# Rotary halves on VectorE, norm factors behind the products, and the second block's two attentions in one pipeline of heads

## The reference, cut to what matters

```python
def rmsnorm(x, g):
    y = xf * lax.rsqrt(jnp.mean(xf * xf, axis=-1, keepdims=True) + EPS)
    return (y * g.astype(F32)).astype(x.dtype)

def rope(x, pos):                     # x1, x2: the two halves of a head's features
    return jnp.concatenate([x1 * cos - x2 * sin, x1 * sin + x2 * cos], axis=-1)

# block two, mixer: two attentions over one normed input, then gates
x = rms_norm(x, final_g of block one);  h = rmsnorm(x, attn_norm)
q_lat, kv_lat, k_pe, q, k, v, gates = split(h @ w_in)
mla  = attention(rmsnorm(q_lat) @ w_uq, rmsnorm(kv_lat) @ w_ukv, rope on 64 of 192 features)
moba = attention(rope(q), rope(k), v)       # 256 tokens are one block: plain causal
y = sigmoid(gate_a) * (mla @ w_o_mla) + sigmoid(gate_b) * (moba @ w_o_moba)
x = x + y @ w_out
```

## Time and profile before

| | |
|---|---|
| runs | 3199.83, 3199.21, 3197.68 us |
| the profiled execution | 3198.27 us, span 3196.6 us |
| TensorE matmul busy | 2965.3 us, 93% of the span |
| VectorE, ScalarE busy | 899.9 us (28%), 464.0 us (15%) |
| mean granted TensorE clock | 0.966 of full |
| DMA engines, whole span | 184 GB/s read from HBM |

### The profile page before, as it was taken

One profiled execution on the slowest core, in us unless ns is written; L12 is line 12 of the kernel. 1 busy time (PEld: TensorE's weight loads), 2 busy tenths in 40 slices (PEclk: granted clock), 3 DMA queues, 4 the chain that ended last, 5 costly groups with the idle time before them and its releaser, 6 DMA issues. The chain is left out here.

```text
span 3196.6 us, 34077 instructions
## 1 busy us (share of the span) xinstructions
PE 2965.3 (93%) x14305; PEld 2290.9 (72%) x14305; DVE 899.9 (28%) x1928; ACT 464.0 (15%) x863; POOL 0.2 (0%) x4
## 2 busy tenths in 40 slices
PE   7998899999898997789999988899899699999997
PEld 6887788888787886568888877799788343443443
DVE  2117511111153112222015414255401322222232
ACT  1001400000042000122000002234300101001001
POOL 0000000000000000000000000000000000000000
PEclk9999999999999999899999999899899799999999
DMA  7443244444343442135544443244252599999996
GB/s 235 157 145 132 67 144 158 145 158 149 101 118 119 158 146 90 48 87 131 132 157 134 157 119 81 80 119 119 80 151 90 238 426 426 427 426 426 426 427 255
DMA packets 358885, 590.24 MB, mean 185 GB/s; under 512 B 11376, under 2 KB 315120, under 8 KB 336112
## 3 DMA queue, kind: packets, MB, share of 16 engines
q1 hardware_dynamic: 358064, 586.22, 51.7%
q10 hardware_dynamic: 704, 2.32, 0.2%
HBM read 587.46 MB, written 1.05 MB: 184 GB/s over the span
## 5 line engine op out<-in xcount | busy, mean ns | idle before, releaser
L642 PE MATMUL bank<-hR,ring 128*128 128x256 f32 x3520 | 763.5, 380 | 8.6 <-DVE hR L405 5.6
L642 PEld LDWEIGHTS bank<-hR,ring 128*128 128x128 f32 x3520 | 670.5, 191 | 100.7 <-issue 7.1
L778 PE MATMUL bank<-big,ring 128*128 128x256 f32 x2016 | 440.3, 382 | 4.9 <-ACT big L957 4.3
L778 PEld LDWEIGHTS bank<-big,ring 128*128 128x128 f32 x2016 | 386.1, 192 | 58.3 <-issue 4.7
L2461 PE MATMUL bank<-ring,wk 128*64 128x512 f32 x1408 | 312.7, 597 | 7.8 <-DMA ring<-in_w_expert_gate 7.8
L2461 PEld LDWEIGHTS bank<-ring,wk 128*64 128x64 f32 x1408 | 99.7, 138 | 213.8 <-issue 213.8
L677 DVE TENSOR_TENSOR wk<-bank,rstd 128x512 f32<-128x512 f32 x88 | 60.9, 692 | 484.3 <-PE bank L642 483.9
L1052 PE MATMUL bank<-hT,ring 128*128 128x256 f32 x768 | 178.7, 393 | 18.6 <-DVEq L2674 18.1
L1052 PEld LDWEIGHTS bank<-hT,ring 128*128 128x128 f32 x768 | 150.3, 198 | 43.6 <-DVEq L2674 19.3
L2487 PE MATMUL bank<-big,wk 128*64 128x512 f32 x352 | 155.8, 595 | 15.1 <-ACT wk L2513 15.1
L814 DVE SCALAR_TENSOR_TENSOR xT<-bank,xT 128x512 f32<-128x512 f32 x36 | 24.9, 692 | 459.4 <-PE bank L778 459.4
(11 more groups left out here) (369 smaller groups left out, 2680.5 us busy)
## 6 DMA issues: line engine op xcount, KB each, us to landing
ring<-in_ffn_w_in SPq DMA_DIRECT2D x88, 1024.0 KB
ring<-in_w_expert_gate SPq DMA_DIRECT2D x44, 2048.0 KB
ring<-in_w_expert_up SPq DMA_DIRECT2D x44, 2048.0 KB
ring<-in_w_in SPq DMA_DIRECT2D x96, 512.0 KB
big<-in_w_expert_down SPq DMA_DIRECT2D x44, 1024.0 KB
ring<-in_ffn_w_out SPq DMA_DIRECT2D x20, 2048.0 KB
ring<-in_w_up SPq DMA_DIRECT2D x22, 1024.0 KB
hR<-in_w_expert_down SPq DMA_DIRECT2D x22, 1024.0 KB
```

Of the source, the lines that this page charges most:

```text
L642: last = nc.tensor.matmul(k.bank[:, n % 4, h * S:(h + 1) * S], w[:, c, h * 256 + m * P:h * 256 + (m + 1) * P], k.hR[:, c, :], start=c == 0 ...
L778: return nc.tensor.matmul(k.bank[:, 4 + o // 2, (o % 2) * S:(o % 2 + 1) * S], w[:, c, o * P:(o + 1) * P], self.src[:, n, :], start=n == 0 ...
```

## The change

- Rotation matrices and their products go. VectorE reads q and k from PSUM, multiplies by cos, and the new `rotated` writes each half times sin into the other half's partitions: 2 instructions for halves of 64 (moba) and for Mla's 64 rotary features, 4 for halves of 32 (diff). ScalarE's copy of q and k for the rotation goes too.
- Norm factors behind the products. Latent, Stick and diff read `hR`. q and k are multiplied by the factor as they leave PSUM (Stick), through the angles (`ScaledAngles`, diff), v through a column of factors made by two one-row products (`column`) and taken by ScalarE as a scale (two instructions in place of one). The convolution's first chunk reads `hR` in part and is scaled behind. moba and the rest read `hT`, which is made meanwhile and announced by `t_ready`.
- `FinalThenNorm` takes one root over both factors and one reciprocal; `finish` makes `hT`, the other reciprocal and the scaled `xT`, in `Latent.dve` (block two) or behind the third head's rope (block three).
- `Attentions` runs a list of heads as one pipeline: moba's eight, then Mla's eight in block two, diff's eight in block three. The order of a pass is now: project the next head, transpose this one, scores of the next, `attend` of this one. The latents' norm is spread through the first two heads.
- `fill`: behind the last head's scores TensorE does the first two gate products of `Merge` (block two), the step sizes (block three's attention), or those gate products ahead of the last transposes (SSD).
- Barriers go behind the norms, Latent, Mla, moba and Merge (Stick's and SSD's stay); `Project` behind `Merge` waits per chunk.

```diff
+def rotated(v, chain, out, src, sin, half):
+    for a in range(0, src.shape[0], half):
+        upper = (a // half) % 2
+        b = a - half if upper else a + half
+        chain.mark(v.scalar_tensor_tensor(out[b:b + half], src[a:a + half], -1.0 if upper else 1.0, sin[a:a + half],
+                                          ALU.mult, ALU.mult))
+    chain.settle()
...
 class FinalThenNorm(Norm):
...
+        second, first = k.both[:, 0:S], k.both[:, S:2 * S]
+        chain(v.tensor_scalar(first, k.bank[:, 4, 0:S], 1.0 / DM, EPS6, ALU.mult, ALU.add))
+        chain(v.tensor_scalar(second, first, EPS6, None, ALU.mult))
+        chain(v.scalar_tensor_tensor(second, k.bank[:, 5, 0:S], 1.0 / DM, second, ALU.mult, ALU.add), self.mean_ready)
         dve.wait_ge(self.root_ready, self.at(self.root_ready, 1))
+        chain(v.reciprocal(second, second), self.rstd_ready)
...
+    def finish(self, dve, chain):
         for b in range(4):
+            v.tensor_tensor(k.hT[:, 2 * b:2 * b + 2, :], k.hR[:, 2 * b:2 * b + 2, :], over(second, 2), ALU.mult)\
+             .then_inc(self.t_ready, 1)
+        chain(v.reciprocal(first, first))
         for c in range(KC):
+            chain.mark(v.scalar_tensor_tensor(k.xT[:, c, :], k.xT[:, c, :], k.p(self.final, c), first, ALU.mult, ALU.mult))
...
 class ConvModule(Stage):
...
+                elif c == 1:
+                    pe.wait_ge(norm.t_ready, norm.at(norm.t_ready, 4))
...
+                                                w[:, q, h * 256 + m * P:h * 256 + (m + 1) * P], (k.hT if c else k.hR)[:, q, :],
...
 class Roped(Softmax):
...
+    def rope(self, dve, g, chain):
+        dve.wait_ge(self.qk_ready, self.at(self.qk_ready, g + 1))
+        self.prior(dve, self.s_ready, g - 1)
+        raw, t1, out = pair(k.bank[:, 0, :]), pair(k.wk[:, self.T1:self.T1 + 2 * S]), pair(self.qk(g))
+        chain.mark(nc.vector.tensor_tensor(t1, raw, over(self.cos, 2), ALU.mult))
+        rotated(nc.vector, chain, out, raw, over(self.sin, 2), self.half)
+        chain(nc.vector.tensor_tensor(out, out, t1, ALU.add), self.rope_done)
...
+class Attentions(Stage):
...
     def pe(self, pe):
+        part, g = self.heads[0]
...
+        part.project(pe, g)
+        if self.lat:
+            self.lat.sums(pe)
+        part.scores(pe, g)
+        for n, (part, g) in enumerate(self.heads):
+            if n + 1 < len(self.heads):
+                after, h = self.heads[n + 1]
+                after.project(pe, h)
+                part.turn(pe, g)
+                after.scores(pe, h)
+            else:
+                pe.wait_ge(part.v_taken, part.at(part.v_taken, g + 1))
+                self.fill(pe)
+                part.turn(pe, g)
+            part.weigh(pe, g)
...
     def dve(self, dve, chain):
+        part, g = self.heads[0]
+        part.rope(dve, g, chain)
+        if self.lat:
+            self.lat.variance(dve, chain)
+        for n, (part, g) in enumerate(self.heads):
+            part.soft_max(dve, g, chain)
+            part.soft_div(dve, g, chain)
+            if n + 1 < len(self.heads):
+                after, h = self.heads[n + 1]
+                after.rope(dve, h, chain)
+            if n == 1:
+                self.late(dve, chain)
...
 class Ssd(Stage):
...
-        self.dt.project(pe)
         self.sub.sums(pe)
...
+        pe.wait_ge(self.copied, 2 * self.G)
+        self.fill(pe)
         pe.wait_ge(self.yt_taken, self.G - 1)
         turn_y(self.G - 1)
...
+    plan = [norm, lat, moba, mla, Attentions(k, "att2", [moba, mla], merge.gates, lat.scale, lat), merge,
+            Project(k, "out2", mt, KC, a["w_out_2"][0], by=merge)]
...
+    plan = [norm, ScaledAngles(k, "ang", norm), diff, dt, Attentions(k, "att3", [diff], dt.project, norm.finish), sub, ssd, merge,
+            Project(k, "out3", mt, KC, a["w_out_3"][0], by=merge),
```

More of the change, by code:

```diff
@@ L878, in pe @@
         k, nc = self.k, self.k.nc
+        norm = self.norm
         for j in range(4):
@@ L1139, in pe @@
         self.project_qk(pe, 0)
+        self.norm.sum(pe)
         self.project_v(pe, 0)
+        self.norm.column(pe)
         scores(0)
@@ L1435, in angle, with __init__, qk_free @@
-    def angle(self, name):
-        return name if not isinstance(name, str) else self.k.c(name)
+    TOTAL = {**Softmax.TOTAL, "qk_taken": 0}
+    fence = False
+    def __init__(self, k, name, norm, h, w, q0, k0, v0, comp, scale, half, cos, sin, out):
+        super().__init__(k, name, norm, h, w, q0, k0, v0)
+        self.COMP, self.SCALE, self.half, self.cos, self.sin, self.OUT = comp, scale, half, cos, sin, out
+    def qk_free(self, g):
+        return self.rope_done, self.at(self.rope_done, g)
@@ new lines, in project, with scores @@
+    def project(self, pe, g):
+        self.project_qk(pe, g)
+        if g == 0 and self.h is self.k.hR:
+            self.norm.sum(pe)
+        self.project_v(pe, g)
+        if g == 0 and self.h is self.k.hR:
+            self.norm.column(pe)
+    def scores(self, pe, g):
+        k, nc = self.k, self.k.nc
+        pe.wait_ge(self.rope_done, self.at(self.rope_done, g + 1))
+        self.prior(pe, self.max_ready, g)
+        d = P // self.COMP
+        for n in range(self.COMP):
+            q, kk = self.qk(g)[n * d:(n + 1) * d, 0:S], self.qk(g)[n * d:(n + 1) * d, S:2 * S]
+            nc.tensor.matmul(k.bank[:, 3 + n, 0:P], q[:, 0:P], kk[:, 0:P], start=True, stop=True)
+            last = nc.tensor.matmul(k.bank[:, 3 + n, P:TRI], q[:, P:S], kk, start=True, stop=True)
+        last.then_inc(self.s_ready, 1)
@@ L1517, in dve, with scale @@
+    def scale(self, dve, chain):
+        k, nc = self.k, self.k.nc
+        inv = self.row(self.INV)
         dve.wait_ge(self.root_ready, self.at(self.root_ready, 1))
-        inv = k.wk[:, 4608:4608 + 2 * S]
-        chain(nc.vector.reciprocal(inv, k.wk[:, 4096:4096 + 2 * S]))
+        chain(nc.vector.reciprocal(inv, self.row(self.VAR)))
+        chain(nc.vector.tensor_tensor(pair(inv), pair(inv), over(self.norm.factor(), 2), ALU.mult))
         for c in range(5):
@@ L1623, in dve @@
[L1623 to L1640 removed]
+        j, h = g // 2, g % 2
@@ new lines, in project @@
+        if g == 0:
+            pe.wait_ge(self.lat.lat_done, 1)
+        if h == 0:
+            pe.wait_ge(self.loaded(j), self.loads(j))
+        s = self.slot_of(j)
+        uq, ukv = k.slot(s, 0, 3, 384), k.slot(s, 1152, 2, 512)
+        self.prior(pe, self.qk_taken, g)
+        self.prior(pe, self.rope_done, g)
+        self.prior(pe, self.v_taken, g)
+        for t in range(T):
+            for c in range(2):
+                last = nc.tensor.matmul(k.bank[:, 1, t * P:(t + 1) * P], kvlat[:, c, t * P:(t + 1) * P],
+                                        ukv[:, c, h * 256 + P:(h + 1) * 256], start=c == 0, stop=c == 1)
@@ L1673, in sp, with part, gates @@
                     sp.dma_start(dst, src).then_inc(self.loaded(j), UNIT_INC // len(parts))
+    def part(self, c, u, n):
+        k, nc = self.k, self.k.nc
+        half, src, w, col = self.parts(c)[u][n]
+        v, chunks = self.view(c * self.per + u, n, src.shape[1]), src.shape[1]
+        out = k.bank[:, 2 * (c % 2) + half // 2, (half % 2) * S:(half % 2 + 1) * S]
+        for q in range(chunks):
+            last = nc.tensor.matmul(out, v[:, q, :], src[:, q, :], start=q == 0, stop=q == chunks - 1)
+        return last
+    def gates(self, pe):
+        pe.wait_ge(self.loaded(0), self.loads(0))
+        for n in range(2):
+            self.part(0, 0, n)
     def pe(self, pe):
-        k, nc = self.k, self.k.nc
+        k = self.k
+        if self.heads:
+            pe.wait_ge(self.heads.o_taken, self.heads.at(self.heads.o_taken, self.heads.G))
         for c in range(KC):
@@ L1681, in pe @@
                 j = c * self.per + u
-                pe.wait_ge(self.loaded(j), self.loads(j))
-                for n, (half, src, w, col) in enumerate(parts):
-                    v, chunks = self.view(j, n, src.shape[1]), src.shape[1]
-                    out = k.bank[:, 2 * (c % 2) + half // 2, (half % 2) * S:(half % 2 + 1) * S]
-                    for q in range(chunks):
-                        last = nc.tensor.matmul(out, v[:, q, :], src[:, q, :], start=q == 0, stop=q == chunks - 1)
+                if c or u:
+                    pe.wait_ge(self.loaded(j), self.loads(j))
+                for n in range(0 if c or u else 2, len(parts)):
+                    last = self.part(c, u, n)
                 last.then_inc(k.w_used, 1)
```

492 lines of the change are left out of this document (249 added, 243 removed).

## The result

The changed kernel takes 3090.93 us (median of four runs, 3088.23 to 3093.06) against 3199.34 us before, measured beside it (four runs). The ratio is 0.9662, interval [0.9647, 0.9677]. The forecast was 3079 us, so of the 119.8 us announced 108.4 came: the time is inside the range and 12 us above the forecast. The profiled execution took 3088.23 us with a span of 3086.4 us.

A forecast was written before the change was run, and what follows sets the result against it. TensorE was taken to set the end nearly everywhere, with gains in attention and convolution gaps. Seven terms sum to 119.8 us off 3198.27, giving 3078.5; with 0.9 for the median, 3079 us, range 3060 to 3108.

The forecast's parts named there:

- convolution: Convolution stage: products start before the norm's factor is ready, first tap 8.0 us earlier, 1 off for the clock; 7 us saved.
- Stick: Stick's start: factor hidden behind the v products, first scores at 869.4 instead of 881.78; 12.4 us saved.
- block two to Merge's second chunk: Block two, norm through moba and Mla: Merge's second chunk starts at 1476.8 instead of 1544.06; 66 us saved after clock allowance.
- diff: Block three's attention: passes of 13.2 us instead of 14.24, one of 18.0 for `finish`; 20 us saved.
- start of SSD: From diff's last scores to SSD's first projection: 18.0 us instead of 22.7; 4.7 us saved.
- end of SSD: Gap ahead of SSD's last transposes: filled by gate products that were due anyway; 5.4 us saved.
- Mla's passes: Block two's Mla heads: 9.5 us each, with TensorE standing 1.5 us where it stood 1.53.
- first scores of block two: Block two's start: Latent starts at 1257.8, TensorE waits 2.3 us for the squares, first scores done at 1297.7.
- moba's passes: Block two's moba heads: 12.4 us each instead of 13.84, the rope with 1 us to spare.
- The pieces of `rotated`: VectorE's rotation in the ropes: each piece costs 0.69 us without overlap; 64x256 takes 0.42.
- rival with doubled pieces: VectorE becomes the bound of the heads: a piece costs twice as much, 32 us more, 3110 us; chance 0.13.
- the joined pipeline does less: Block two and other heads: misplaced latents' norm or `finish` holds passes, or uncovered copies keep pass lengths; 3100 us; chance 0.09.

The follow-up runs named there:

- x10: Changed kernel with Stick's first projection of q and k waiting for the norm's factor, the multiplications by it kept: 3102.12 us.
- x5: Changed kernel with `rotated` issued twice in moba's and diff's ropes, doubling the cost of a piece there: 3127.57 us.
- x1: Changed kernel plus three dummy products (1.3 us, unused bank) per Mla pass, in the gap ahead of the wait for Mla's scores: 3073.13 us.
- x2: Changed kernel with the wait for ScalarE's copy of q and k ahead of the transposes in Mla passes, splitting the gap in two: 3084.26 us.
- x12: Changed kernel plus three dummy products (1.3 us) behind each of Mla's scores, so the gap ahead of scores stays: 3086.73 us.
- x6: Changed kernel with block three's `finish` cut into six pieces, each ahead of a rope in diff: 3082.46 us.
- x7: Changed kernel with the fills undone: `fill` behind the last head's product with v, in SSD behind the last transposes: 3103.48 us.
- x3: Changed kernel with Mla's roped part projected first and signalled by itself, v last: 3059.21 us.
- x4: Changed kernel with this head's product with v ahead of the next head's scores in passes that project an Mla head: 3068.47 us.
- x9: Changed kernel with x3 and x6 together: 3052.80 us.
- x11: x9 with the sums of block three's sub-norm put behind SSD's first projection: 3052.16 us.

## Why the prediction was right, and where 12 us went

Term by term, as forecast and as the profile after measures it:

| step | forecast, us | measured, us |
|---|---|---|
| convolution | 7 | 7.7 |
| Stick | 12.4 | 12.6 |
| block two to Merge's second chunk | 66 | 53.7 |
| Merge to Project, both blocks | 4.3 | 4.6 |
| diff | 20 | 18.0 |
| start of SSD | 4.7 | 4.2 |
| end of SSD | 5.4 | 7.7 |
| the rest of the kernel | 0 | 1.6 |
| sum | 119.8 | 110.0 |

(Profiled executions: 3198.27-3088.23 = 110.0; the rows are rounded.)

The mechanism was right in its parts, and one term was too large. That the total came within 12 us is in part luck: Mla's passes alone took 14.5 us more than said, and about 1.2 us more at a slow clock behind them, while SSD's end, the first scores of block two and the rest of the kernel gave some 5 us that the forecast hadn't claimed. Of the rest, 1.3 us lie behind the last `Project`, where TensorE waits 4.70 us for the first expert's weights in place of 7.83.

- **Convolution and Stick** came as worked out: the eight products and the column hide the factor. The first tap starts 15.3 us behind the end of the products (266.17-250.87), forecast 15.0. Stick's share was tested by x10.
- **Up to block two's first scores** it is 39.8 us (1275.73-1235.89), forecast 41.3. TensorE waits 2.02 us for the squares, forecast 2.3, and for nothing else. The clock doesn't fall over that gap: 80 records take 17.57 us, 0.22 each. The 1 us set aside for it wasn't needed.
- **moba's passes** are 12.3 us (forecast 12.4), with 0.8 us to spare by x5 (forecast 1.0). The latents' norm delays nothing.
- **Mla's passes are the step that failed**, in "TensorE stands 1.5 us where it stood 1.53". The gap is 1.48 us, and at full clock a pass takes 9.42, both as forecast. But from the last moba head's product with v at 1361.12 to Mla's last at 1451.63, eight passes take 90.5 us, forecast 76. I carried the full clock over from the kernel before, where the clock was 0.99 with 1.53 us of idling in a pass of 10.15 us (1368.03-1357.88), but in two gaps, of 0.95 and 0.58 us, 1 us apart. In a shorter pass and with one gap it didn't hold: 0.80. x1 gives the price: at the full clock eight passes take 75.4 us in place of 90.5, in spite of 1.3 us of work added to each. x2 brings the two pieces back and x12 the longer pass; each holds the clock up more of the time (0.85 and 0.96), neither all of it. I had counted clock losses only behind single gaps of 2 us and more.
- **diff**: a pass is 13.13 us, forecast 13.2, and waits for the rope as said. `finish` costs one pass of 17.95 us between starts of scores, as said, and, what I left out, the pass behind it, 14.88 us with products at a slow clock: 6.6 us in all where 4.8 were forecast. The first pass takes 15.1 us, forecast 14.2. By x6 spreading `finish` gives back 6.4 us of its 6.6.
- **SSD**: at the start 2.41 us of waiting for the squares stand, forecast 2.5; the step sizes run at the higher clock (3.66 us), the sums at the lower (6.98). The end gave 2.3 us more than said. TensorE came through the gates at the higher clock where it had stood 5.43 us; x7 has the gap and the slow clock behind it (9.56 us for 32 records in place of 7.93) back.
- **The pieces of `rotated`** take 0.71 us (diff) and 0.43 (Mla, two in 0.86), 0.02 and 0.01 more than a plain operation of as many columns, without overlap, so crossing partitions costs next to nothing. The rival with doubled pieces was the experiment x5: a doubled piece costs 36 us in moba and diff alone, not 32 in all heads. The windows put it down to the clock at least in part (0.88 in place of 0.95). The Trainium skill's rule of the held instruction (VectorE: DVE Perf Modes, "Two Vector instructions with no wait between them") agrees with the trace: 0.71 us from piece to piece in diff, where `hT`'s multiplications, which stay on their partitions, take 2.50/4 = 0.62; no run changed only that. An operation from PSUM (L1486) and one from SBUF (L1488) both take 0.69 us, so the surcharge that the Trainium skill states for PSUM (VectorE: DVE Perf Modes, "The TRN2 errata — SBUF-src ops pay a fixed extra latency per instruction") isn't seen in this trace.
- **The rivals.** No piece costs twice as much, so VectorE didn't become the bound in the rival's way, though diff's pass does wait for the rope, as forecast; nor did late norms or slow pieces occur. 3091 lies between the forecast and "the joined pipeline does less" (3100), but not by its mechanism.

What stays open: which pattern of work and gaps drops the clock. Per pass at full clock, the gaps and the clean passes out of seven were 1.48 us in 9.42 (one clean), 1.41 in two pieces in 9.43 (four clean), 1.48 in 10.72 (five clean), 0.87 in 8.84 (all) and 0.18 in 9.42 (all). In the kernel before it was 1.53 in two pieces in 10.15 (clock 0.99). At a pass of 9.4 us less idling goes with a clock that holds, and so does a longer pass around the same gap, but each case rests on one profiled execution, and no rule is shown.

## What to carry to other kernels

When a change shortens a loop pass but leaves its gap, ask for TensorE's clock again: a pass with the same wait and less work around it can lose more to the clock than to the wait. The better remedy here was order, not filler. Project first what has the longest way back (x3, 32 us), or put a ready product into the gap (x4, 23 us); dummy products gave 18. Side work for VectorE belongs in pieces in front of what it waits for anyway, since one lump of 7.5 us cost 6.4 by x6 although VectorE was busy for only 30% of the span.

## What the runs showed of the hardware

- Adding 24 useless products, three in each of eight Mla heads (10.4 us of work), made the kernel 18.3 us faster inside the gaps and 4.7 us faster outside them (medians; 15.4 and 2.3 between the traces). The same gap of 1.48 us left the granted clock at 0.80 or 0.96, depending on the work around it.
- A window's busy share hides this: 70.67 us of 81 busy with the clock at 0.80, and 70.66 with 0.96.
- 16 products of a single column (32 records) take 6.98 us behind a wait of 2.41 us, at a granted clock of 0.50, and 3.63 us behind a long projection, at 1.00 (x9, x11).
- VectorE operations that read 32 partitions and write another 32 take 0.71 us for 512 columns, against 0.69 for a plain one on 128.
